# Tokens and first weights in quarters, column halves at the ends of stages, products of high parts at their beginnings, in a two-block fp32 model kernel

## The chip, the cores and the metric

One Trainium2 chip, of which the kernel uses one core. The metric is the device time of one execution in microseconds, median of a few runs. TensorE multiplies, VectorE and ScalarE work on elements, GpSimd does small odd jobs, SyncE issues most transfers. Each engine takes its instructions in order, and engines wait for each other on semaphores.

## What is computed

256 tokens of width 1024, all in float32, go through two models of two layers each. The first model: a convolution mixer, a gated linear recurrence, and after each a mixture of 16 experts of which a token takes 2. The second: forgetting attention (16 heads) and dilated attention (3 groups of 8 heads), and after each a feed-forward part with a width-3 convolution.

```python
for layer in (0, 1):                         # first model
    m = conv_mixer(x) if layer == 0 else rglru_mixer(x)
    x = layer_norm(4**0.25 * x + m)
    f = moe(x)        # softmax router, best group of 4, top 2; silu(x@w1) * (x@w3) @ w2
    x = layer_norm(4**0.25 * x + f)
h = rms_norm(x); x = x + forgetting_attention(h @ w_qkv, log_sigmoid(h @ w_f + b)) @ w_out
x = x + conv_ffn(rms_norm(x))                # second model
kv = rms_norm(x) @ w_kv; q = rms_norm(x) @ w_q
x = x + dilated_attention(q, kv) @ w_out
x = x + conv_ffn(rms_norm(x))
return rms_norm(x)
# conv_ffn: u = causal_conv3(h @ w_up) + b; a, g = split(u); (silu(g) * a) @ w_down
```

## The kernel before, in words

The work is a fixed sequence of stages: ew_in, ew_out (mixer of layer 0), moe0, ow_in, gates, ow_out (recurrence), moe1, aq/av, aw_out (attention), up0, down0, wk, bwq, wv, bw_out (dilated attention), up1, down1. All weights come from HBM once, in chunks of 1 MB (128 partitions x 2048 floats), 541 of them in the order of `STREAM` (L39). They go into a ring of 12 slots and 11 extra slots that other buffers leave free at times; `sync_load` (L303) has SyncE issue each load as soon as the slot's previous chunk is released (`released`, L283). For the experts the release is the last product with a chunk, for dense stages the split of its last quarter.

**Three products for one.** Dense stages keep float32 precision on a faster format: a weight piece of 512 columns (a quarter of a chunk) is rounded by ScalarE to a high part (`scalar_split`, L317, signal w_hi), and VectorE subtracts it to get the low part (`vector_split`, L325, w_lo). The activations are split likewise (x_hi, x_lo). `three` (L343) then multiplies low x high, high x low and high x high into one PSUM bank. Four pieces are held split; TensorE signals w_used for a piece, and only then the piece four further on may be split. `tensor_features` (L352) makes 256 output features of all tokens with a chunk: two halves j, each 8 x 3 = 24 products of 256 columns. `tensor_out` (L383) and, for its last part, `tensor_out_last` (L400) make an output projection with 512 columns a product: two token halves m, two column halves d. The last 24 products are the end of an output stage.

**Expert stages** multiply the float32 chunks directly (L1012), in the order in which they land.

**Between stages.** After ew_out and ow_out VectorE adds the residual by token half and column half (`vector_residual`, L611), gathers statistics and has GpSimd raise the variance to the power -0.5 (`pool_rstd`, L442); the halves are normalised (token half 0 on ScalarE, 1 on VectorE), turned by TensorE (`tensor_norm_features`, L495) and, ahead of od and fg, scaled and split in quarters q (`scalar_normed_split`, L553, and `vector_normed_split`, L568). Before the attention and feed-forward stages the factor of the rms norm goes onto a diagonal (`vector_rms`, L639, signal diag) and TensorE turns and scales at once (`tensor_to_features`, L508): token half 0, then half 1, into banks 4 to 7. The sum of squares comes from one ScalarE instruction over 1024 columns (`scalar_rms`, L629).

**The order around the change.** In the first stage SyncE loads x as two token halves (`sync_setup`, L676), then ten chunks; TensorE turns half 0, then half 1; ScalarE splits all four pieces of chunk 0 before it takes any high part of x, then VectorE the low parts; ScalarE also requests the constants `cols` (L670). At the beginning of any stage the first product waits for x_lo. In `forget_tensor` (L1767) the 24 products for the gate's logits come first and wait for all of x_lo. `vector_after_experts` (L1303) splits pieces 0 and 1, then does statistics and norm. In `tensor_out_last` the loop is m, then kk (the two contraction blocks), then d, so for each token half the first column half is done after 9 of 12 products. At the end `vector_finish` (L2478) applies factor and gain to a whole token half in one instruction, and `sync_store` stores it.

## Time and profile before

| | us |
|---|---|
| median of 3 runs (lowest, highest) | 1844.25 (1841.64, 1846.14) |
| the profiled execution's own time | 1845.43 |
| its span, first to last instruction | 1844.2 |
| TensorE busy in it | 1718.9 (93%) |
| VectorE busy | 797.8 (43%) |
| ScalarE busy | 614.8 (33%) |
| GpSimd busy | 119.8 (6%) |
| read from HBM | 542.19 MB, 295 GB/s over the span |

The busy share says how much of the span an engine had something in hand, not whether it set the pace: in the expert stages TensorE is busy nearly all the time and yet may run behind a stream of weights. For a question about one stage the stretch is to be read: who waits for whom there, the share of the DMA engines, and the clock that TensorE was granted (1.00 is 2.4 GHz, 0.50 is 1.2 GHz).

### The profile page before, as it was taken

To read this page: it belongs to the slowest core of one execution; us is meant where nothing else is said; L and a number is where in the kernel's file an instruction comes from. 1 tells how busy PE (TensorE), PEld (TensorE's weight loads), DVE (VectorE), ACT (ScalarE), POOL (GpSimd) and SP (SyncE) were. 2 spreads that over 40 slices of the span, in tenths; PEclk is the share of its full clock that TensorE was granted. 3 is DMA by queue.
4 is the path that set the end of the run, shared out by engine and by line. 5 is a ranking of instruction groups with operands and counts; after the bars stand their busy time and mean duration, and the time that the engine had idled before them with its cause. 6 is when DMAs were issued, how large, how long until landed. Compare 5 with 4: busy or idle time off the path is not lost.

```text
span 1844.2 us, 23747 instructions
## 1 busy us (share of the span) xinstructions
PE 1718.9 (93%) x9906; PEld 1115.7 (61%) x9906; DVE 797.8 (43%) x1534; ACT 614.8 (33%) x1157; POOL 119.8 (6%) x143
## 2 busy tenths in 40 slices
PE   8978999999997988999999988799999999999998
PEld 7954444333233974334432332777999889779986
DVE  5962111110003673111110001766788667758885
ACT  5531010000002551001000001456666554656664
POOL 0000000000000000000000000033111001501110
PEclk9989999999999988999999999999999999999999
DMA  9449999999999549999999999434455544335550
GB/s 398 186 189 377 423 422 422 424 423 420 420 419 419 225 168 383 424 422 424 421 422 423 420 420 420 187 123 144 147 184 182 193 159 163 125 125 184 183 183 24
DMA packets 75378, 544.88 MB, mean 295 GB/s; under 512 B 8448, under 2 KB 8448, under 8 KB 9472
## 3 DMA queue, kind: packets, MB, share of 16 engines
q1 hardware_dynamic: 74592, 541.10, 73.6%
q10 hardware_dynamic: 672, 2.18, 0.3%
q8 instruction: 82, 1.34, 0.3%
q14 instruction: 32, 0.26, 0.0%
HBM read 542.19 MB, written 1.05 MB: 295 GB/s over the span
## 4 chain that ended last, share of the span: by engine, by line
PE 68%; DMA 18%; DVE 8%; ACT 3%; issue 1%; POOL 1%; SPq 0%; ACTq 0%; DVEq 0%
PE PS L1012 24%; DMA ring<-in_w 12%; PE PS L346 12%; PE PS L348 11%; PE PS L347 11%; DMA F<-in_w 3%; PE PS L989 2%; PE PS L1024 2%; DVE wl L329 2%; DMA ring<-in_a_w_in 2%; DMA ring<-in_odd_w_in 1%; PE PS L737 1%; ACT wh L323 1%; DVE X L619 1%; PE PS L1038 0%
## 5 line engine op out<-in xcount | busy, mean ns | idle before, releaser
L1012 PE MATMUL PS<-ring,F 128*64 128x512 f32 x2112 | 477.7, 597 | 38.6 <-DMA ring<-in_w 33.8
L329 DVE TENSOR_TENSOR wl<-ring,wh 128x512 fp32r<-128x512 f32 x512 | 368.1, 739 | 189.5 <-ACT wh L323 186.8
L323 ACT ACTIVATE wh<-ring 128x512 fp32r<-128x512 f32 x512 | 319.8, 630 | 299.7 <-PE PS L348 292.0
L346 PE MATMUL PS<-xh,wl 128*128 128x256 f32 x1216 | 353.7, 291 | 10.7 <-DVE xl L834 3.8
L1012 PEld LDWEIGHTS PS<-ring,F 128*64 128x64 f32 x2112 | 143.6, 137 | 355.3 <-issue 258.9
L347 PE MATMUL PS<-xl,wh 128*128 128x256 f32 x1216 | 346.6, 285 | 0.0
L348 PE MATMUL PS<-xh,wh 128*128 128x256 f32 x1216 | 346.5, 285 | 0.0
L346 PEld LDWEIGHTS PS<-xh,wl 128*128 128x128 f32 x1216 | 235.5, 194 | 15.3 <-issue 5.7
L347 PEld LDWEIGHTS PS<-xl,wh 128*128 128x128 f32 x1216 | 235.7, 194 | 0.6
L348 PEld LDWEIGHTS PS<-xh,wh 128*128 128x128 f32 x1216 | 235.5, 194 | 0.0
L346 PE MATMUL PS<-wh,xl 128*128 128x512 f32 x360 | 148.1, 411 | 13.1 <-DVE xl L435 6.0
L348 PE MATMUL PS<-wh,xh 128*128 128x512 f32 x360 | 143.2, 398 | 0.0
L347 PE MATMUL PS<-wl,xh 128*128 128x512 f32 x360 | 143.1, 397 | 0.0
L1301 DVE COPY F<-PS 64x512 f32<-64x512 f32 x32 | 22.2, 695 | 270.7 <-PE PS L1012 270.7
L1280 DVE SCALAR_TENSOR_TENSOR F<-F,PS 128x512 f32<-128x512 f32 x32 | 22.0, 688 | 229.3 <-ACT F L1129 229.3
L1012 PE MATMUL PS<-F 128*64 128x512 f32 x480 | 109.3, 597 | 3.4 <-DMA F<-in_w 2.4
L1285 DVE SCALAR_TENSOR_TENSOR F<-F,PS 128x512 f32<-128x512 f32 x32 | 22.0, 688 | 205.3 <-PE PS L1012 205.3
L1147 ACT ACTIVATE F<-PS 64x512 f32<-64x512 f32 x32 | 18.9, 590 | 233.6 <-PE PS L1012 233.6
L1129 ACT ACTIVATE F<-PS 128x512 f32<-128x512 f32 x32 | 19.1, 597 | 231.6 <-PE PS L1012 231.6
L346 PEld LDWEIGHTS PS<-wh,xl 128*128 128x128 f32 x360 | 69.4, 193 | 32.3 <-DVE xl L435 11.8
L348 PEld LDWEIGHTS PS<-wh,xh 128*128 128x128 f32 x360 | 69.2, 192 | 15.2
L1141 ACT ACTIVATE F<-PS 128x512 f32<-128x512 f32 x32 | 19.0, 595 | 177.4 <-PE PS L1038 177.4
(353 smaller groups left out, 1760.6 us busy)
## 6 DMA issues: line engine op xcount, KB each, us to landing
ring<-in_w SPq DMA_DIRECT2D x264, 1024.0 KB, 26.4
F<-in_w SPq DMA_DIRECT2D x60, 1024.0 KB, 25.2
ring<-in_ffn_up SPq DMA_DIRECT2D x44, 1024.0 KB, 4.9
early<-in_w SPq DMA_DIRECT2D x40, 1024.0 KB, 25.8
ring<-in_ffn_down SPq DMA_DIRECT2D x22, 1024.0 KB, 4.8
ring<-in_even_w_in SPq DMA_DIRECT2D x10, 1024.0 KB, 17.0
Z<-in_w SPq DMA_DIRECT2D x10, 1024.0 KB, 23.4
XT<-in_w SPq DMA_DIRECT2D x10, 1024.0 KB, 24.1
```

The lines of the kernel that those rows point to most:

```text
L323: act.e.activation(self.wh[:, p % NPIECE, :], self.piece_source(p), ACT.Copy).then_inc(*self.up("w_hi", p))
L329: dve.e.tensor_tensor(self.wl[:, p % NPIECE, :], self.piece_source(p), f32(self.wh[:, p % NPIECE, :]), ALU.subtract).then_inc(*self.up("w_ ...
L346: e.matmul(out, left[1], right[0], start=first, stop=False)
L347: e.matmul(out, left[0], right[1], start=False, stop=False)
L348: return e.matmul(out, left[0], right[0], start=False, stop=last)
L989: t = pe.e.matmul(self.PS[:, 6 + half, k4 * 128:k4 * 128 + 128], self.X[:, h, k * 128:k * 128 + 128], v["S"][:, h, :], start=(h == 0), sto ...
L1012: t = pe.e.matmul(PS[64 * half:64 * half + 64, bank, :], lhs(k), weights[:, a:a + 512], start=(k == 0), stop=(k == 7))
L1024: t = pe.e.matmul(self.PS[:, b, :], v["Gt"][:, h, d, :], v["Y"][d], start=(q == 0), stop=(q == 7))
L1129: act.e.activation(v["hh"], PS[:, 4, :], ACT.Tanh, scale=0.5).then_inc(*up("tanh", layer, ex))
L1280: e.scalar_tensor_tensor(out=v["hh"], in0=v["hh"], scalar=1.0, in1=PS[:, 4, :], op0=ALU.add, op1=ALU.mult).then_inc(*up("silu", layer, ex))
L1285: e.scalar_tensor_tensor(out=v["hh"], in0=v["hh"], scalar=0.5, in1=PS[:, 5, :], op0=ALU.mult, op1=ALU.mult).then_inc(*up("hidden", layer, ex))
L1301: e.tensor_copy(v["Y"][1 - o][64:128, :], PS[64:128, 5, :]).then_inc(*up("y1", layer, ex))
```

## The change

Five edits.

1. **The start.** x comes as four column quarters of both token halves, chunk 0 as its four pieces, in the order tokens 0, piece 0, tokens 1 to 3, pieces 1 to 3, each on its own semaphore. TensorE turns quarter by quarter. ScalarE and VectorE split piece 0, take quarters 0 to 2 of x, piece 1, quarter 3, pieces 2 and 3. The constants are computed by VectorE after the split of piece 7 (in `constants`), not before that of piece 4. The first block of features goes to bank 6.
2. **First block of a stage.** With `first`, the 24 products of j = 0 run as 16 products with the high part of x (both weight parts), which wait for x_hi and w_lo, then 8 with its low part, which wait for x_lo. It is used at the beginnings of the first stage, od, fg, kv, up0 and up1; up0 and up1 use bank 0 for it. In fg the logits follow block 0.
3. **Splits ahead of od and fg.** ScalarE takes high part 1 before it normalises quarter 2. VectorE splits pieces 2 and 3 before and after the norm instead of between the low parts.
4. **Column halves.** `tensor_out_last` runs d outside kk, so a column half is done after 6 of 12 products. Squares are taken by column halves, and one VectorE instruction adds the two sums and epsilon. VectorE adds column half 0 of token half 1 before it waits for the factor of token half 0.
5. **The end.** VectorE multiplies by the gain before the factor is known; ScalarE applies the factor to columns 0 to 511, VectorE to the rest; four stores of 0.25 MB take the place of two of 0.5 MB.

```diff
-    def tensor_features(self, stage, p, bank):
+    def tensor_first_features(self, stage, p, out, xh, xl):
+        pe = self.pe
+        for k in range(8):
+            h, l = self.weight(p + k // 4)
+            a = slice(k % 4 * 128, k % 4 * 128 + 128)
+            pe.wait_ge(self.at("x_hi", stage, k // 2), self.at("w_lo", p + k // 4))
+            pe.e.matmul(out, l[:, a], xh[:, k, :], start=k == 0, stop=False)
+            pe.e.matmul(out, h[:, a], xh[:, k, :], start=False, stop=False)
+        for k in range(8):
+            h, l = self.weight(p + k // 4)
+            a = slice(k % 4 * 128, k % 4 * 128 + 128)
+            pe.wait_ge(self.at("x_lo", stage, k // 2))
+            t = pe.e.matmul(out, h[:, a], xl[:, k, :], start=False, stop=k == 7)
+            if k % 4 == 3:
+                t.then_inc(*self.up("w_used", p + k // 4))
+                yield p + k // 4
+    def tensor_features(self, stage, p, bank, first=False):
         pe, PS = self.pe, self.PS
         xh, xl = self.left.get(stage, (self.xh, self.xl))
         for j in range(2):
+            if first and j == 0:
+                yield from self.tensor_first_features(stage, p, PS[:, bank, 0:256], xh, xl)
+                continue
...
         for m in range(2):
             x = slice(m * 128, m * 128 + 128)
-            for kk in range(2):
-                k = nk - 2 + kk
-                for d in range(2):
+            for d in range(2):
+                for kk in range(2):
+                    k = nk - 2 + kk
...
         self.scalar_normed(stage, n, 0)
         high(0)
+        high(1)
         self.scalar_normed(stage, n, 2)
-        for q in (1, 2, 3):
-            high(q)
-    def vector_normed_split(self, stage, n, to, pieces):
+        high(2)
+        high(3)
+    def vector_normed_split(self, stage, n, to):
         dve = self.dve
         self.vector_normed(stage, n, 1)
         low(0)
         self.vector_normed(stage, n, 3)
-        low(1)
-        for p in pieces:
-            self.vector_split(p)
-        low(2)
-        low(3)
+        for q in (1, 2, 3):
+            low(q)
...
-        if src_stage:
-            act.wait_ge(self.at("resid", src_stage, h, 0), self.at("resid", src_stage, h, 1))
-        else:
-            act.wait_ge(self.at("x_final", h))
-        act.e.activation(self.Z[:, h, :], self.X[:, h, :], ACT.Square, scale=1.0 / 32,
-                         accum_out=self.sm[:, 430 + h:431 + h]).then_inc(*self.up("square", stage, h))
+        for d in range(2):
+            c = slice(d * 512, d * 512 + 512)
+            act.wait_ge(self.at("resid", src_stage, h, d) if src_stage else self.at("x_final", h))
+            act.e.activation(self.Z[:, h, c], self.X[:, h, c], ACT.Square, scale=1.0 / 32,
+                             accum_out=self.sm[:, 430 + 2 * h + d:431 + 2 * h + d]).then_inc(*self.up("square", stage, h, d))
+    def vector_rms_sum(self, stage, h):
+        self.dve.wait_ge(self.at("square", stage, h, 1))
+        self.dve.e.tensor_scalar(self.sm[:, 490 + h:491 + h], self.sm[:, 430 + 2 * h:431 + 2 * h],
+                                 self.sm[:, 431 + 2 * h:432 + 2 * h], RMS_EPS, ALU.add, ALU.add).then_inc(
+            *self.up("var_eps", (stage, h)))
     def vector_rms(self, stage, h):
         dve = self.dve
-        dve.wait_ge(self.at("square", stage, h))
-        self.vector_rstd(self.sm[:, 430 + h:431 + h], RMS_EPS, h, (stage, h))
         dve.wait_ge(self.at("rstd", (stage, h)))
         dve.e.tensor_scalar(self.Z[:, h, 0:128], self.ident[:, :], self.sm[:, 500 + h:501 + h], None,
                             ALU.mult).then_inc(*self.up("diag", stage, h))
+    def vector_out_rms(self, stage, p, nk):
+        self.vector_residual(stage, p, nk, 0, 1.0, self.X)
+        self.vector_rms_sum(stage, 0)
+        self.vector_residual(stage, p, nk, 1, 1.0, self.X, halves=(0,))
+        self.vector_rms(stage, 0)
+        self.vector_residual(stage, p, nk, 1, 1.0, self.X, halves=(1,))
+        self.vector_rms_sum(stage, 1)
+        self.vector_rms(stage, 1)
...
     def sync_setup(self):
-        for h in range(2):
-            self.sp.e.dma_start(self.X[:, h, :], self.A["x"][h * 128:h * 128 + 128, :]).then_inc(self.x_in[h][0], 16)
+        x, w = self.A["x"].rearrange("(h p) d -> p h d", h=2), self.source(0)
+        def tokens(q):
+            s = slice(256 * q, 256 * q + 256)
+            self.sp.e.dma_start(self.X[:, :, s], x[:, :, s]).then_inc(self.x_in[q][0], 16)
+        def piece(j):
+            s = slice(PIECE * j, PIECE * j + PIECE)
+            self.sp.e.dma_start(self.chunk(0)[:, s], w[:, s]).then_inc(self.first_in[j][0], 16)
+        tokens(0)
+        piece(0)
+        for q in (1, 2, 3):
+            tokens(q)
+        for j in (1, 2, 3):
+            piece(j)
...
+        pe.wait_ge(at("consts", "ident"))
+        for q in range(4):
+            pe.wait_ge(self.x_in[q])
+            for h in range(2):
+                for j in range(2):
+                    k = 2 * q + j
+                    t = pe.e.transpose(PS[:, q, j * 256 + h * 128:j * 256 + h * 128 + 128],
+                                       self.X[:, h, k * 128:k * 128 + 128], self.ident[:, :])
+            t.then_inc(*up("turned", "ev", q))
         p, conv = PIECES["ew_in"], 0
         for c in range(10):
             if c < 4:
-                pe.wait_ge(at("x_lo", "ev", c))
+                pe.wait_ge(at("x_hi" if c == 0 else "x_lo", "ev", c))
             elif c >= 6:
                 pe.wait_ge(self.even_bank_read((0, 1, 4, 5)[c - 6]))
-            for _ in self.tensor_features("ev", p + 4 * c, (0, 1, 2, 3, 4, 5, 0, 1, 4, 5)[c]):
+            for _ in self.tensor_features("ev", p + 4 * c, (6, 1, 2, 3, 4, 5, 0, 1, 4, 5)[c], c == 0):
...
     def even_scalar(self):
         act, at, up, v = self.act, self.at, self.up, self.even_views()
-        for n in range(NPIECE):
+        for q in range(4):
+            if q in (0, 3):
+                self.scalar_split(q // 3)
+            act.wait_ge(at("turned", "ev", q))
+            act.e.activation(self.xh[:, 2 * q:2 * q + 2, :], self.bank2(q), ACT.Copy).then_inc(*up("x_hi", "ev", q))
+        for n in (2, 3):
             self.scalar_split(n)
         self.scalar_setup()
-        for q in range(4):
-            act.wait_ge(at("turned", "ev", q))
-            act.e.activation(self.xh[:, 2 * q:2 * q + 2, :], self.bank2(q), ACT.Copy).then_inc(*up("x_hi", "ev", q))
...
-        for n in range(NPIECE):
-            self.vector_split(n)
         for q in range(4):
+            if q in (0, 3):
+                self.vector_split(q // 3)
             dve.wait_ge(at("x_hi", "ev", q))
             dve.e.tensor_tensor(self.xl[:, 2 * q:2 * q + 2, :], self.bank2(q), f32(self.xh[:, 2 * q:2 * q + 2, :]),
                                 ALU.subtract).then_inc(*up("x_lo", "ev", q))
-        dve.wait_ge(self.cols_in)
-        dve.wait_ge(at("ev_pad"), at("ev_consts", "bh"))
+        for n in (2, 3):
+            self.vector_split(n)
+        def constants():
...
+                if (c, j) == (0, 3):
+                    constants()
...
             self.vector_moments(stage, h)
+        self.vector_split(p + 2)
         self.vector_norm(stage)
+        self.vector_split(p + 3)
...
-        pe.wait_ge(at("wf_lo"))
-        for k in range(8):
-            pe.wait_ge(at("x_lo", "fg", k // 2), at("x_lo", "fg", 3))
-            a = slice(k * 48, k * 48 + 48)
-            t = self.three(PS[0:48, 7, 0:256], (self.wfh[:, a], self.wfl[:, a]), (self.xh[:, k, :], self.xl[:, k, :]),
-                           k == 0, k == 7)
-        t.then_inc(*up("fg_logits"))
         p0 = self.forget_slots()
         for c in range(2):
-            for p in self.tensor_features("fg", p0 - 8 + 4 * c, c):
+            for p in self.tensor_features("fg", p0 - 8 + 4 * c, c, c == 0):
                 self.forget_tensor_slot(p - p0)
+            if c == 0:
+                self.forget_logits()
...
+        if stage != "down1":
+            for h in range(2):
+                self.scalar_rms(stage, stage, h)
+            return
+        self.scalar_rms(stage, stage, 0)
+        self.scalar_finish(0)
+        self.scalar_rms(stage, stage, 1)
+        self.scalar_finish(1)
...
+    def ffn_bank(self, n):
+        return 4 + n % 4 if n else 0
...
+            pe.wait_ge(at("taps", layer, n - 4) if n >= 4 else at("x_lo" if n else "x_hi", stage, n))
+            for _ in self.tensor_features(stage, p + 4 * n, self.ffn_bank(n), n == 0):
...
-    def vector_finish(self, h):
+    def vector_finish(self, p, nk):
         dve, at, up = self.dve, self.at, self.up
-        dve.wait_ge(at("square", "down1", h))
-        self.vector_rstd(self.sm[:, 430 + h:431 + h], RMS_EPS, h, ("down1", h))
-        dve.wait_ge(at("rstd", ("down1", h)), (self.s_row, 48))
-        dve.e.scalar_tensor_tensor(out=self.Z[:, h, :], in0=self.X[:, h, :], scalar=self.sm[:, 500 + h:501 + h],
-                                   in1=self.F[:, 12288:13312], op0=ALU.mult, op1=ALU.mult).then_inc(*up("y_ready", h))
+        G = self.F[:, 12288:13312]
+        def gain(h, d):
+            c = slice(d * 512, d * 512 + 512)
+            dve.wait_ge((self.s_row, 48), at("resid", "down1", h, d), at("square", "down1", h, d))
+            dve.e.tensor_tensor(self.Z[:, h, c], self.X[:, h, c], G[:, c], ALU.mult).then_inc(*up("y_gain", h, d))
+        def scale(h):
+            dve.wait_ge(at("rstd", ("down1", h)), at("y_gain", h, 1))
+            dve.e.tensor_scalar(self.Z[:, h, 512:1024], self.Z[:, h, 512:1024], self.sm[:, 500 + h:501 + h], None,
+                                ALU.mult).then_inc(*up("y_ready1", h))
+        self.vector_residual("down1", p, nk, 0, 1.0, self.X)
+        self.vector_rms_sum("down1", 0)
+        gain(0, 0)
+        gain(0, 1)
+        self.vector_residual("down1", p, nk, 1, 1.0, self.X, halves=(0,))
+        scale(0)
+        self.vector_residual("down1", p, nk, 1, 1.0, self.X, halves=(1,))
+        gain(1, 0)
+        self.vector_rms_sum("down1", 1)
+        gain(1, 1)
+        scale(1)
...
+    def scalar_finish(self, h):
+        act, at, up = self.act, self.at, self.up
+        act.wait_ge(at("rstd", ("down1", h)), at("y_gain", h, 0))
+        act.e.activation(self.Z[:, h, 0:512], self.Z[:, h, 0:512], ACT.Copy,
+                         scale=self.sm[:, 500 + h:501 + h]).then_inc(*up("y_ready0", h))
     def sync_store(self):
         for h in range(2):
-            self.sp.wait_ge(self.at("y_ready", h))
-            self.sp.e.dma_start(self.out[h * 128:h * 128 + 128, :], self.Z[:, h, :]).then_inc(self.s_out, 16)
-        self.sp.e.wait_ge(self.s_out, 32)
+            for d in range(2):
+                c = slice(d * 512, d * 512 + 512)
+                self.sp.wait_ge(self.at(f"y_ready{d}", h))
+                self.sp.e.dma_start(self.out[h * 128:h * 128 + 128, c], self.Z[:, h, c]).then_inc(self.s_out, 16)
+        self.sp.e.wait_ge(self.s_out, 64)
...
```

## Rows read from the trace of the kernel before

**Rows 1.** Page, part 4: the chain that ended last, by engine
```profile
PE 68%; DMA 18%; DVE 8%; ACT 3%; issue 1%; POOL 1%; SPq 0%; ACTq 0%; DVEq 0%
```

**Rows 2.** Stretches: busy by engine (count); last three: TensorE's clock, DMA share, GB/s
```profile
60.00:116.00 56.00, 50.03 (x306) 44.99 (x305) 45.05 (x96) 27.44 (x52) 0.72 (x1) 0.93 0.22 76
150.00:152.00 2.00, 2.00 (x12) 0.72 (x10) 0.00 (x0) 0.00 (x0) 0.00 (x0) 1.00 0.09 37
158.00:580.00 422.00, 402.21 (x1896) 150.57 (x1892) 48.44 (x109) 39.22 (x68) 0.00 (x0) 1.00 1.01 421
...
718.00:720.00 2.00, 2.00 (x11) 0.62 (x8) 0.00 (x0) 0.00 (x0) 0.00 (x0) 1.00 0.56 90
722.00:1151.00 429.00, 405.32 (x1904) 151.25 (x1904) 50.03 (x113) 37.04 (x65) 0.42 (x1) 1.00 1.01 419
...
600.00:610.00 10.00, 10.00 (x85) 10.00 (x85) 6.68 (x13) 6.16 (x11) 0.00 (x0) 1.00 0.99 411
```

**Rows 3.** Timeline, first 20 us: start, us, engine, line, operation, count [idle <- releaser]
```profile
4.63 3.64 PE L524 MATMUL PS<-ident,X 128*128 128x128 f32 x16 [4.63 <-DMA X<-in_x]
8.26 0.63 ACT L323 ACTIVATE wh<-ring 128x512 fp32r<-128x512 f32 x1 [6.17 <-DMA ring<-in_even_w_in]
12.07 0.58 PE L346 MATMUL PS<-xh,wl 128*128 128x256 f32 x1 [3.80 <-DVE xl L834]
16.55 0.17 DVE L837 TENSOR_SCALAR sm<-cols 128x4 f32<-128x4 f32 x1 [2.74 <-DMA cols<-in_cols]
```

**Rows 4.** Stretches as in rows 2, around beginnings of stages, for the clock
```profile
12.07:16.10 4.03, 4.03 (x19) 4.03 (x20) 1.74 (x3) 0.95 (x2) 0.00 (x0) 1.00 1.01 422
593.10:599.95 6.85, 6.55 (x29) 6.29 (x30) 3.79 (x6) 1.49 (x3) 0.00 (x0) 0.50 1.02 420
1163.40:1169.90 6.50, 4.72 (x23) 4.41 (x24) 3.99 (x5) 0.00 (x0) 0.00 (x0) 0.50 0.57 205
1487.20:1494.00 6.80, 4.22 (x33) 3.75 (x33) 4.14 (x10) 4.08 (x10) 0.76 (x2) 1.00 0.03 13
```

**Rows 5.** Timeline of VectorE, end of ew_out
```profile
123.87 0.69 DVE L621 SCALAR_TENSOR_TENSOR Z<-X,PS 128x512 f32<-128x512 f32 x1 [0.78 <-PE PS L348]
```

**Rows 6.** Timeline, beginning of od
```profile
587.37 1.53 DVE L474 TENSOR_SCALAR Z<-PS,sm 128x512 f32<-128x512 f32 x2 [0.68 <-POOL sm L444]
593.01 1.29 DVE L329 TENSOR_TENSOR wl<-ring,wh 128x512 fp32r<-128x512 f32 x2
591.67 1.66 ACT L560 ACTIVATE xh<-XT 128x512 fp32r<-128x512 f32 x3
587.84 1.97 PE L503 MATMUL PS<-ident,Z 128*128 128x128 f32 x16 [2.48 <-ACT Z L492]
597.54 0.41 PE L348 MATMUL PS<-xh,wh 128*128 128x256 f32 x1
```

**Rows 7.** Timeline of TensorE, beginning of fg
```profile
1165.18 0.42 PE L346 MATMUL PS<-xh,wfl 128*48 128x256 f32 x1 [5.91 <-DVE xl L575]
```

**Rows 8.** Timeline, end of down0: first and last of its last 24 products, then the tail
```profile
1481.74 0.39 PE L346 MATMUL PS<-wh,xl 128*128 128x512 f32 x1
1486.95 0.39 PE L348 MATMUL PS<-wh,xh 128*128 128x512 f32 x1
1489.07 2.02 PE L522 MATMUL PS<-Z,X 128*128 128x128 f32 x16 [1.73 <-DVE X L619]
1491.36 2.05 PE L522 MATMUL PS<-Z,X 128*128 128x128 f32 x16 [0.27 <-DVE Z L644]
1483.98 1.37 DVE L619 TENSOR_TENSOR X<-X,PS 128x512 f32<-128x512 f32 x2 [0.68 <-PE PS L348]
1491.02 0.29 DVE L644 TENSOR_SCALAR Z<-ident,sm 128x128 f32<-128x128 f32 x1 [0.67 <-POOL sm L444]
```

**Rows 9.** Timeline, the last instruction of VectorE; and the store's time to landing
```profile
1840.21 1.28 DVE L2483 SCALAR_TENSOR_TENSOR Z<-X,sm,F 128x1024 f32<-128x1024 f32 x1 [0.67 <-POOL sm L444]
DMA to landing us min/median/max: 2.6/2.6/2.6
```

70 lines of the change are left out of this document (35 added, 35 removed).

## The prediction

> **What bounds the kernel now.** I began with the chain that ended last: 68% of the span is TensorE and 18% DMA [rows 1]. The reader should then ask, stretch by stretch, which of the two sets the pace. In the stretches of the experts the DMA share is full for 422 and 429 us at 421 and 419 GB/s [rows 2]: whatever TensorE gains inside them is worth nothing, and they move only if the stream of weights begins earlier. Between them and after them the stream is nearly idle or has room (0.22 of it is used at 60 to 116 us [rows 2]), and TensorE and the small chains between two stages set the time. The change touches only those: the first 20 us, the ends of stages, and their beginnings.
>
> Does a gain ahead of an expert stretch reach the end? The stream stalls just before each saturated stretch, because every slot is full until the first expert frees one: 0.91 of 150 to 152 us is idle (1.8 us), and 0.44 of 718 to 720 us (0.9 us) [rows 2]. All its later loads are released by TensorE's progress. So what the even and the odd stage gain moves the whole stream, and what only the tail between the last fill and the first expert gains (0.68 us, below) fits into those idle times. I count both in full.
>
> **The first stage.** Now: the first half of the tokens (0.5 MB) lands at 4.6 us, the first weight chunk (2 MB in all by then) at 8.2 us, TensorE turns tokens for 3.64 us and then idles 3.80 us until the first low part of x exists, at 12.07 [rows 3]. With eight transfers of 0.25 MB in the order of the diff, and the same rate (1.5 MB in 3.6 us, so 0.6 us for a quarter), tokens land at 4.0, 5.2, 5.8, 6.4 and the pieces at 4.6, 7.0, 7.6, 8.2 us. Sixteen transposes at 3.64/16 = 0.23 us, four for a quarter, end at 8.0 us (TensorE is the late one, not the DMA). The high parts and piece 0's split hide under them: ScalarE and VectorE have nothing else there. Products then start at about 8.1 instead of 12.07: 4.0 us. Further, the clock. The rows print a granted clock of 1.00 from the start, but 19 products took 4.03 us at 12.07 (0.212 each) [rows 4], where transposes of later stages go at 1.97/16 = 0.12 [rows 6]: the first is the pace of 1.2 GHz, the second that of 2.4. The pace rose after 4.03 us of unbroken work. In the new order TensorE is busy without a break from 5.2 us (second quarter), so I let it rise at 9.3 us: 6 slow products instead of 19, 13 x 0.09 = 1.2 us. Sum 5.2 us. Bounds: 2 us, if the smaller transfers are a good deal slower, and 6 us.
>
> The Trainium skill speaks to this: "TensorE: Matmul & The Clock Gate", section "Part 1: The HAM clock gate", says that the warm-up is an amount of time with activity and not a number of matmuls. By that rule it is right that the transposes count; if only the products counted, the 1.2 us would go.
>
> What it adds: the request for the constants (cols) now stands behind the fourth split in ScalarE's queue, which waits for piece 3 (8.2 us, where it now waits for the chunk, 8.2 us as well), so it goes out when it did and lands near 16.5 us as before [rows 3]. VectorE meets that wait after the split of piece 7 instead of before that of piece 4. Behind it stands piece 8, due when TensorE ends the second block of columns at about 20 us; cover 2.5 us. Pieces 0 and 1 are given back at products 20 and 24 instead of 12 and 24; their successors are needed at product 48, 28 x 0.12 = 3.4 us later, and a release costs two splits, some 2 us. Both at nothing; gone, each would cost about 1 us per us late.
>
> **The ends of ew_out and ow_out (column halves one by one).** VectorE is the late one: from 123.87 us, when the first half is done [rows 5], it has sums and statistics without a gap (as the timeline goes on) up to the factor of the norm. In the last 24 products the first half is done after 6 instead of 9. At (1486.95 - 1481.74)/23 = 0.2265 us for a product [rows 8] the whole VectorE chain starts 0.68 us earlier; its second half is due after 12 products as before, which then just meets it. Twice 0.68 = 1.4 us. The piece with number 2 is now wanted after 3 products instead of 6; it was split two pieces' time before, and I find some room. Cost 0, at worst 0.3 each (half a split).
>
> **The beginnings of od and fg.** In od transposes end at 589.81 (587.84 + 1.97); ScalarE ends the last high parts at 593.3, the 24th product starts at 597.54 [rows 6]. The two weight splits that stood between the low parts go elsewhere: one into the 0.68 us in which VectorE waits for GpSimd ahead of the norm [rows 6] (the pair in the way took 1.29, so one fits: free), one into the wait for the transposes. ScalarE's sum is unchanged, so the last high part comes at 593.4, 12 products are left then, and VectorE's low parts, with no splits between, follow the high parts by one operation of some 0.7 and are ready at 594.3, before they are due. At 0.12 us the 24 are done at 594.9, 2.9 us earlier than 597.75, and 10 products that ran slow before 599.95 run fast: 3.7 us. But the granted clock was 0.50 in 593.10 to 599.95 [rows 4], after a thin stretch from 589.81. If it falls again, the 24 are done at 593.4 + 12 x 0.212 = 595.95: 8.5 products ahead, 1.0 us if it rises when it did, 2.3 if sooner; I take 1.5.
>
> In fg TensorE idles 5.91 us until 1165.18, as the logits of the forget gate want all low parts, and then runs 23 products in 6.5 us at a clock of 0.50 [rows 4, 7]. Now block 0 comes first, on high parts, and the logits second, so 24 products are done by 1159.27 + 3.6 (as in od) + 12 x 0.12 = 1164.3, where the 24th used to end near 1170: 5.5 us. If the clock falls: 1165.4, and at 1169.9 about 23 products ahead, x 0.12 = 2.8; I take 3.0. Nothing of block 1 is late by it: behind the low parts VectorE multiplies in the gains as before, now some 5 us earlier.
>
> Does the clock fall? Before, the thin stretch was 3.3 us empty but for 6 products, then two more waits (od), and 5.9 us empty (fg). Now it is 3.5 us with 12 to 16 products in it in each. That is about as thin as what held the clock elsewhere (the rms tails, idle for 1.73 us [rows 8], kept 1.00 [rows 4]). I take it that it falls in one of the two: 3.7 + 3.0 or 1.5 + 5.5, so 6.9 us.
>
> **The three rms tails (aw_out, down0, bw_out) and the beginnings behind them.** Now VectorE adds token half 0 at 1483.98 (0.43 after the start of the 9th product), waits for its square and factor, and only then adds half 1, so TensorE starts turning at 1489.07 though the last product started at 1486.95 [rows 8]. New: half 1's last column half is added at 1486.95 + 0.43, 0.69 long (half of 1.37): 1488.07; TensorE starts 0.15 later, 1488.22, and is through half 0 after 2.02 us at 1490.24. The factor of half 1 took 2.1 us from the sum to its diagonal (1489.07 - 0.15 to 1491.02 [rows 8]); squaring halves as they come shortens that, so it is there by 1490.1. TensorE itself is then the late one: 1491.36 becomes 1490.24, 1.12 us. Behind it the first block starts on high parts, but VectorE's splits of pieces 2 and 3 still follow the low parts, as in the code of before, and are due at the end of the 24: 0.2 us. Three times 1.32 = 4.0 us.
>
> **The end (down1).** Now the last factor is applied in 1.28 us from 1840.21 and the store takes 2.6 us from issue to landing [rows 9]. New: the last sum ends about 0.6 us earlier (VectorE has gains to multiply in between), the factor is applied by two engines to half a row each (0.6 instead of 1.28, gain 0.7), and the last store is half as large (0.6 us less to move) but is the second of two issued together (0.35 later). Sum 0.6 + 0.7 + 0.3 = 1.6 us; bounds 0.5 and 2.5. The skill's "DMA: Bandwidth & Descriptors", section "Anatomy of one DMA", fits 2.0 us plus the bytes at 436 GB/s to a transfer; an estimate by that page puts the half store 0.6 us below the whole, as I do.
>
> **Sum.** 5.2 + 1.4 + 6.9 + 4.0 + 1.6 = 19.1 us. The profiled execution took 1845.4 (span 1844.2 and 1.2 around it), 1.2 over the median of the three; it would come to 1826.3, the median to 1844.25 - 19.1 = 1825.
>
> **Rivals.** (a) The clock holds in od and fg: 3.7 + 5.5, so 21.4 and 1823. (b) It falls in both: 4.5, so 16.7 and 1827.5. (c) Small transfers are slower, 1.0 us a quarter: the start gives 3, 1827. (d) They don't overlap at all. Each of the eight takes the 2.6 us that a store shows [rows 9]; the last piece lands at 22 us, block 0 ends at 25 instead of 19.6, and the start loses 5.4: 1835.7. For it: nothing in the trace; against it: 2 MB by 8.2 us [rows 3] is full overlap. It is what the rule to batch transfers to 1 MiB or more in the skill's "DMA: Bandwidth & Descriptors", section "Measured (HBM→SBUF, 128 partitions, SWDGE, issued from GpSimd)", would make of it at its worst. (e) The heads bring nothing, since low parts or splits are as late as before (the diff doesn't do what it says): minus 7.5, 1832.6. Against it: the splits between the low parts are gone. (f) The expert stream doesn't move: all gains ahead of it are lost (5.2 + 1.4 + 2.6): 1834.3. Against it: its idle times in [rows 2]. (g) Slower: the stream, always full, settles at a lower rate, because the loads meet TensorE's releases in another rhythm. It covers 851 us; it eats the 19.1 and 5.5 more from 851/(851 + 24.6) x 420 = 408 GB/s on. Ten microseconds in a later full part show 411 [rows 2], so such a rate exists; none lasts.
>
> **How the numbers follow.** A measurement of this kernel tells some 0.3% (5.5 us) from no change. Chances: forecast 0.38, (a) 0.24, (b) 0.18, (c) 0.06, (d) 0.02, (e) 0.05, (f) 0.05, (g) 0.02. All but (g) lie under 1838.7, so faster 0.96, same 0.02, slower 0.02. Range: from 1821 (a, with 2 us for the spread of runs and the upper bounds) to 1832 (b and c with the lower bounds of start and end, and half of e): 0.86 or so.
>
> **What would show it.** The first product at about 8 us and block 1 at 14.4 instead of 19.6; the first expert product some 6 us earlier; the same DMA share in the expert stretches; 24 products done 3.6 + 1.4 us after the transposes in od and fg, with the granted clock beside it; transposes of the rms tails 0.85 us nearer to the last product, and no wait between their halves. It would be wrong if VectorE's wait for the constants reached past 19 us, if a low part turned up as releaser of more than 0.3 us in a beginning, or if the rate of the stream changed.

## The result and the profile after

| | kernel before | kernel after |
|---|---|---|
| median of the runs | 1845.2 us (4 runs, 1841.6 to 1847.3) | 1829.3 us (4 runs, 1826.4 to 1830.8) |
| profiled execution | 1845.4 us (span 1844.2) | 1828.6 us (span 1827.3) |
| mean granted clock in it | 0.985 | 0.987 |

The ratio is 0.9917 (0.9898 to 0.9935): 16 us faster, under 1%, but clear of the spread of the runs. Over all later comparisons, before has a median of 1843.6 us in 35 runs, so 14 to 16 us is the better statement. The forecast was 19.1 us less and a median of 1825, in a range of 1821 to 1832.

Where the two profiled executions reach the same instruction of TensorE (us; lead is how much earlier after is there, new is what it gained since the row above):

| what starts | before | after | lead | new |
|---|---|---|---|---|
| first convolution | 32.75 | 29.55 | 3.2 | 3.2 |
| routing of layer 0 | 133.03 | 127.75 | 5.3 | 2.1 |
| second gather, behind 16 expert products | 153.24 | 149.74 | 3.5 | -1.8 |
| last combination of layer 0 | 581.68 | 578.63 | 3.05 | -0.45 |
| od's first recurrence product | 630.40 | 624.23 | 6.2 | 3.1 |
| routing of layer 1 | 699.59 | 691.25 | 8.3 | 2.2 |
| second gather, layer 1 | 719.81 | 713.23 | 6.6 | -1.8 |
| last combination of layer 1 | 1151.26 | 1144.75 | 6.5 | -0.1 |
| fg, first turning of attention weights | 1205.65 | 1194.37 | 11.3 | 4.8 |
| turning behind down0 | 1489.07 | 1475.58 | 13.5 | 2.2 |
| end of the span | 1844.2 | 1827.3 | 16.9 | 3.4 |

Every change shows where it was made, and in two places time is given back: at the first expert of each layer. TensorE's timeline in the trace of after, at the start of the kernel, where it answers [rows 3], and from the routing of layer 0 to the first expert (start, us, engine, line, operation, count, [idle <- releaser]):

```profile
3.71 1.09 PE L782 MATMUL PS<-ident,X 128*128 128x128 f32 x4 [3.71 <-DMA X<-in_x]
7.34 2.82 PE L782 MATMUL PS<-ident,X 128*128 128x128 f32 x12 [2.54 <-DMA X<-in_x]
9.81 0.56 PE L361 MATMUL PS<-xh,wl 128*128 128x256 f32 x1
13.71 0.28 PE L348 MATMUL PS<-xh,wl 128*128 128x256 f32 x1
...
137.69 0.40 PE L1132 MATMUL PS<-sm,upper 128*128 128x16 f32 x2 [3.57 <-DVE sm L1273]
139.44 3.78 PE L1056 MATMUL PS<-F,X 128*128 128x128 f32 x16
143.91 5.89 PE L1079 MATMUL PS<-F 128*64 128x512 f32 x16 [0.69 <-ACT F L1182]
```

The same place in before:

```profile
142.98 0.61 PE L1065 MATMUL PS<-sm,upper 128*128 128x16 f32 x2 [3.58 <-DVE sm L1206]
149.66 3.65 PE L1012 MATMUL PS<-F 128*64 128x512 f32 x16 [0.69 <-ACT F L1115]
```

The second quarter of the tokens was there only at 7.3 us, where I had 5.2. And the 16 first expert products took 5.89 us instead of 3.65: TensorE idles for 3.6 us in the routing in both kernels, and the granted clock is 0.50 behind it; in before it was back at 1.00 as the expert began, in after it was not. TensorE busy, granted clock, DMA share and GB/s by two microseconds, before and then after:

```profile
148.00:150.00 2.00, 1.31 (x7) 0.65 0.96 406
150.00:152.00 2.00, 2.00 (x12) 1.00 0.09 37
```

```profile
142.00:144.00 2.00, 1.31 (x8) 0.50 1.04 438
144.00:146.00 2.00, 2.00 (x6) 0.50 0.61 258
146.00:148.00 2.00, 2.00 (x6) 0.50 0.02 8
148.00:150.00 2.00, 2.00 (x10) 0.88 0.62 152
```

### The profile page after: what moved, and what is told of

Same layout as the page of the kernel before. It is cut to its first block, busy times and chain, and to the rows that moved or that the text cites. A ratio compares the mean times of both kernels' runs of the same rounds, so it can differ in the third digit from the quotient of the medians.

```text
span 1827.3 us, 23779 instructions
## 1 busy us (share of the span) xinstructions
PE 1717.2 (94%) x9906; PEld 1111.1 (61%) x9906; DVE 799.2 (44%) x1538; ACT 619.0 (34%) x1179; POOL 121.2 (7%) x143
## 3 DMA queue, kind: packets, MB, share of 16 engines
q8 instruction: 82, 1.34, 0.3%
## 4 chain that ended last, share of the span: by engine, by line
PE 70%; DMA 18%; DVE 6%; ACT 3%; issue 1%; POOL 1%; SPq 1%; DVEq 0%; ACTq 0%
PE PS L1079 24%; DMA ring<-in_w 12%; PE PS L348 12%; PE PS L350 11%; PE PS L349 11%; DMA F<-in_w 3%; PE PS L1056 2%; PE PS L1091 2%; DMA ring<-in_a_w_in 2%; DMA ring<-in_odd_w_in 1%; DVE wl L331 1%; PE PS L795 1%; ACT wh L325 1%; PE PS L545 1%; SPq L313 1%
## 5 line engine op out<-in xcount | busy, mean ns | idle before, releaser
L348 PE MATMUL PS<-xh,wl 128*128 128x256 f32 x1168 | 336.4, 288 | 2.7 <-ACT F L1645 1.4
L349 PE MATMUL PS<-xl,wh 128*128 128x256 f32 x1168 | 330.4, 283 | 0.0
L350 PE MATMUL PS<-xh,wh 128*128 128x256 f32 x1168 | 330.3, 283 | 0.0
L348 PEld LDWEIGHTS PS<-xh,wl 128*128 128x128 f32 x1168 | 223.8, 192 | 5.9 <-issue 2.3
L349 PEld LDWEIGHTS PS<-xl,wh 128*128 128x128 f32 x1168 | 223.9, 192 | 0.6
L350 PEld LDWEIGHTS PS<-xh,wh 128*128 128x128 f32 x1168 | 223.9, 192 | 0.0
L1196 ACT ACTIVATE F<-PS 128x512 f32<-128x512 f32 x32 | 19.1, 597 | 236.3 <-PE PS L1079 236.3
L348 PEld LDWEIGHTS PS<-wh,xl 128*128 128x128 f32 x360 | 69.0, 192 | 32.3 <-DVE xl L458 11.9
L350 PEld LDWEIGHTS PS<-wh,xh 128*128 128x128 f32 x360 | 68.9, 191 | 15.1
```

Of the source, the lines that this page charges most:

```text
L348: e.matmul(out, left[1], right[0], start=first, stop=False)
L349: e.matmul(out, left[0], right[1], start=False, stop=False)
L350: return e.matmul(out, left[0], right[0], start=False, stop=last)
L1196: act.e.activation(v["hh"], PS[:, 4, :], ACT.Tanh, scale=0.5).then_inc(*up("tanh", layer, ex))
```

## The experiments

Times within a kernel are read from its one profiled execution; medians are of 4 to 10 runs, beside runs of before on the same chip.

**The start alone.** Before, with the start of after.

> The kernel before with the new start alone (tokens and first weights by quarters, block 0 on high parts first). Theory (the start is worth 3.2 us, and what it gains travels on, less what a clock that is still low takes back): the first convolution product 3.2 us earlier than before (29.7 instead of 32.9), the first expert product 3 to 5 us earlier than 149.66, and the end 1 to 4.8 us earlier, by whether the 16 first expert products take 3.65 us (granted clock back at 1.00) or up to 5.9 (still 0.50). Rival (the stream of expert weights does not move): the end 0 us earlier, with the first expert waiting for a transfer. Rival (it loses in the hand-over to the next stages): the lead at 104 us is under 3.2.

1840.2 us against 1842.5 (ratio 0.9986, 0.9973 to 1.0): by the medians alone the start is worth 0 to 5 us. Within the profiled execution it is plainer. First convolution at 29.52, as in after. First expert at 143.63, six us early, since the clock also kept its 1.00 ahead of the middle of the stage; 16 products in 3.65 us; last combination of layer 0 at 576.28: 5.4 us early. The lead passes through the stream of expert weights. That holds in every kernel tried: from the second gather to the last combination it took 428.2 to 429.6 us in layer 0, for second gathers between 145.3 and 153.2 us.

**Why the start gives 3.2.** Three other ways to load the first 2 MB:

```diff
 e_tok2k:  tokens(0), tokens(1), piece(0), tokens(2), tokens(3), piece(1..3)
+    h, s = q % 2, slice(q // 2 * 512, q // 2 * 512 + 512)   # 2 KB rows
+    dma_start(self.X[:, h, s], x[:, h, s])
 e_tok4k:  tokens by half (4 KB rows) x2, then piece(0..3)   # 2 KB rows
 e_rows4k: tokens by half (4 KB rows) x2, then two pieces at a time (4 KB rows) x2
```

> The kernel after with the tokens still in four transfers of 0.25 MB, but each a token half by a column half (2 KB rows) instead of both token halves by 256 columns (1 KB rows), in the order two, piece 0, two, pieces 1 to 3. Theory (short rows slow the queue down to 100 to 130 GB/s between 3.3 and 5 us): the second pair lands by 5.8 instead of 7.3, the first product starts at about 8.6 instead of 9.8, and the first convolution 1 us earlier than 29.7. Rival (small transfers start slowly whatever their rows, or several share the engines): first product at 9.6 to 10, convolution within 0.3 us of 29.7.

> The kernel after with the tokens in two transfers of 0.5 MB again (one for each token half, 4 KB rows), both ahead of the first weights, which stay in four pieces; the rest as after. Runs so far: 1 KB rows moved at 100 to 130 GB/s from 3.3 to 5 us, 2 KB rows at 170 to 250, and the 4 KB rows of before at 430. Theory (a row costs its engine about the same time whatever its length, so short rows are what took 2 us from the start): the rate is at 400 or more from 3.3 us on, all tokens are there by 6.5 us, TensorE turns them without a gap to 8.4 us, the first product starts near 8.4 and the first convolution near 28.3 instead of 29.55: 1 to 1.3 us gained. Rival (the first weights are then too late): piece 0 lands after 8 us and the first product starts at 9.5 or later, nothing gained.

> The kernel after with rows of 4 KB for all that is loaded first: tokens in two transfers (one for each token half), then the first chunk in two (two pieces each), nothing under 0.5 MB. Runs so far: the rate of the queue fell to 80 to 180 GB/s whenever transfers with rows of 1 or 2 KB began, and was 420 while the 4 KB rows of the tokens moved. Theory (row length): no such dip, 400 GB/s or more from 3.5 us on; tokens there by 6, pieces 0 and 1 by 7.2, 2 and 3 by 8.3 us; first product by 8.6 and no wait for a split behind it; first convolution at 28.3 to 28.9 instead of 29.0 to 29.75. Rival (the dip belongs to the first weights, whatever their rows): it comes again at 5 us, first product at 9.2, a wait behind it, convolution near 32.

The rate of the queues in the first 12 us, 40 slices of 0.3 us, GB/s; before, after, e_tok4k, e_rows4k:

```profile
GB/s 0 0 0 0 0 0 246 55 109 218 355 437 437 437 396 423 382 464 437 410 437 437 382 437 437 437 437 437 437 437 437 437 410 410 437 437 437 410 437 379
```

```profile
GB/s 0 0 0 0 0 0 34 188 362 382 290 130 82 133 116 102 123 219 266 304 335 352 324 294 328 283 236 300 355 396 423 464 457 505 437 437 437 437 410 437
```

```profile
GB/s 0 0 0 0 0 0 27 109 191 314 423 423 410 423 396 423 369 225 253 157 116 164 123 191 225 300 348 362 376 444 437 464 444 437 410 437 437 410 437 410
```

```profile
GB/s 0 0 0 0 0 0 109 177 164 137 341 437 410 423 423 423 437 382 396 341 232 218 341 382 382 423 478 464 451 437 437 410 437 437 437 437 437 437 437 437
```

The dip stands where the first weights begin, not where the short rows of the tokens are. In after the first tokens, in 1 KB rows, moved at 362 to 382 GB/s up to 3.0 us. In the dip (114 GB/s from 3.3 to 5.1 us) most of the bytes are those of piece 0, in 2 KB rows, and from 5.1 to 7.2 us the 1 KB rows of the other tokens moved at 299 GB/s. In e_tok4k the dip comes with the weights' 2 KB rows (176 GB/s from 5.1 to 7.2 us), in e_rows4k with their 4 KB rows (225 from 6.0 to 6.6), and in before, with 8 KB rows, not at all. So the theory that I took into these runs, that the tokens' 1 KB rows are the slow ones, falls. Its rival in the last of them, that the dip belongs to the first weights, holds, with the addition that it is the weaker the longer their rows are. What makes it is open. Outside the dip the length of a row has a small price: a packet of 1, 2, 4 and 8 KB took its engine 46, 84, 159 and 309 ns, which is 356, 390, 412 and 424 GB/s for 16 engines.

The time did not follow the rate. The first product came earlier than the 9.81 us of after, at 9.58 (2 KB tokens), 9.19 and 9.14 us, but the first convolution at 29.75, 32.12 and 30.23 us, where the kernels with the start of after have 28.98 to 29.55; the medians are 1830.1, 1829.4 and 1829.9. In the last two the first piece lands behind all tokens (ScalarE's split at 7.70 and 7.64 instead of 5.79), its low part is what TensorE waits for (1.24 and 0.93 us), and so is that of piece 1 (1.21 and 0.35), which stands in VectorE's queue behind three low parts of x. The clock did more. TensorE's timeline in e_tok4k; then its busy time, granted clock, DMA share and GB/s by four microseconds there, and last the same in after:

```profile
9.19 0.36 PE L361 MATMUL PS<-xh,wl 128*128 128x256 f32 x1 [1.24 <-DVE wl L331]
11.59 0.56 PE L361 MATMUL PS<-xh,wl 128*128 128x256 f32 x1 [1.21 <-DVE wl L331]
```

```profile
8.00:12.00 4.00, 1.60 (x10) 0.86 1.03 421
12.00:16.00 4.00, 4.00 (x21) 0.50 1.02 426
16.00:20.00 4.00, 4.00 (x29) 0.78 1.01 416
```

```profile
12.00:16.00 4.00, 4.00 (x36) 1.00 0.99 416
```

In after the pace was low from the first product, 9.81, to 11.9 us, and then high. In e_tok4k it was high at the first product, fell to 0.50 at 10.9 and came back at 17.7 us. That is 6.1 us of work at half the pace (from 11.59 on) against 2.1, so 2.0 us lost; with the wait of 1.2 and less the start that came 0.6 earlier it makes the 2.6 by which the convolution is late. In e_rows4k, where the pace rose at 13.5 us, the same sum is 0.9 + 0.35 - 0.7, for the 0.7 measured. What the order of after gives is that TensorE works without an idle time from 7.34 us on; that the waits of 1.2 us are what made the clock fall is argued from their place ahead of it.

**Undoing the beginnings, and undoing the ends.** e_heads_old is after with `first` false everywhere but in the first stage, the forget gate's logits ahead of block 0, and splits of pieces 2 and 3 between the low parts; e_tails_old is after with whole-row squares, `for kk ... for d` in the last products of ew_out and ow_out, and the old last scaling and stores.

> The kernel after with the old beginnings of od, fg, the first up products and kv (block 0 waits for low parts, two weight splits between the low parts, the forget gate's logits first); everything else as after. Theory (they are worth 3.1 in od, 4.8 in fg and 0.2 in each of the other three): the run loses 8.5 us, 1838. Of the 1.35 to 1.43 us per rms tail and head, 0.1 to 0.3 is lost. Rival (the beginnings matter little, the gain at od and fg is the clock that fell elsewhere): it loses under 4 us, with the same 24 products in the same time.

> The kernel after with the old ends: squares of whole rows, the factor of half 0 ahead of half 1's sums, the old order in the last products of ew_out and ow_out, the old last scaling and the two whole stores. Theory (0.68 at each of ew_out and ow_out, 1.1 to 1.2 at each of three rms tails, 1.4 at the end): 6.3 us lost, 1835.5. Rival (the tails are worth less, since low parts are what is waited for behind them either way): the 24 products of the next stage start later but end within 0.5 us, and 3 us are lost. Rival (the clock of 0.50 at the first expert products hides what ew_out and ow_out gained): 1.4 of it shows up as nothing, 5 us lost.

Medians 1834.8 us (1833.7 to 1837.0) and 1833.4 us (1830.3 to 1841.2): 5.4 and 4.1 lost, where 8.5 and 6.3 were expected. Runs with this spread can't tell the 6.3 of the ends from their rivals' 5 and 3, so the places decide: fg, from its first transpose to its first decay product, takes 32.3 to 32.5 us in the three kernels with the old beginning and 27.2 to 27.8 in eight of ten with the new one (the others, with fillers, took 28.9 and 30.3, the latter with a stand-still as below): 4.8 us, as expected. od, from its transposes to its first recurrence product, takes 40.8, 42.6 and 43.8 us old, and 38.9 to 41.5 new in all but one run with a stand-still: 2.5 between the means, with the clock fallen in both kinds. In the one pair that differs in the beginnings alone, e_heads_old and after, od differs by 1.3 only (40.8 and 39.5), and with fg's 4.8 and the heads below that makes up the 5.9 us between their profiled executions. So fg's part is sure, and od's lies between 1.3 and the 3.1 of the table. From the turning behind aw_out to that behind down0, one tail and one head, 195.60 us in before, 194.20 in after, 195.43 with the old tails, 194.29 with the old heads: the tail is worth 1.2 to 1.3, the head 0.1 to 0.2. The tail in after, and with the old ends:

```profile
1474.38 0.29 DVE L669 TENSOR_SCALAR Z<-ident,sm 128x128 f32<-128x128 f32 x1
1475.58 3.92 PE L545 MATMUL PS<-Z,X 128*128 128x128 f32 x32 [0.87 <-DVE X L640]
1477.10 0.29 DVE L669 TENSOR_SCALAR Z<-ident,sm 128x128 f32<-128x128 f32 x1 [0.67 <-POOL sm L467]
```

```profile
1485.12 2.02 PE L545 MATMUL PS<-Z,X 128*128 128x128 f32 x16 [1.72 <-DVE X L640]
1487.41 2.05 PE L545 MATMUL PS<-Z,X 128*128 128x128 f32 x16 [0.27 <-DVE Z L665]
```

0.85 us less ahead of the 32 transposes and 0.27 less between them, the 1.12 of the working. The two ends of ew_out and ow_out gave their 0.68 us each: the idle time ahead of the norm's transposes is 1.34 in after and 2.02 in e_start_only and in e_tails_old.

**Holding the clock.** TensorE turns the identity (or multiplies it by ones) into bank 7, which nobody reads, instead of idling.

```diff
+    def tensor_fill(self, n):            # e_fill, e_fill_start, e_route_fill
+        for _ in range(n):
+            self.pe.e.transpose(self.PS[:, 7, 0:128], self.ident[:, :], self.ident[:, :])
+    def tensor_fill(self):               # e_route_long, e_both
+        for _ in range(7):
+            self.pe.e.matmul(self.PS[:, 7, 0:256], self.ident[:, :], self.ones[:, :], ...)
 moe_tensor_route, ahead of the wait for "chosen":
+        self.tensor_fill(27)             # 30 in e_route_fill
 tensor_norm_features("ln1"), ("ln3"):
+        self.tensor_fill(18)             # e_fill and e_fill_start only
```

> The kernel after with TensorE turning the identity into a bank that nobody reads while it would wait: 27 such transposes in each routing (behind the tokens' transposes), 18 ahead of the norm's transposes for od and for fg. Theory (the time given back at the first experts, and the slow beginnings of od and fg, are the clock that fell in those waits): the granted clock stays at 1.00 there; the gather takes 2.0 instead of 3.8 us, the first 16 expert products 3.65 instead of 5.89 and 5.61, the norm's transposes 1.97 instead of 3.14 and 2.83, and fg's 24 first products 2.2 us less. Up to 4.7 us in each routing, 1 in od, 3 in fg: 13 us below the kernel after, some 1816. Rival 1 (transposes of one small operand do not hold the clock): same time as after, 1829, clock still 0.50. Rival 2 (the clock holds, but the stream of expert weights is then what is late): expert products wait for transfers, and only od's and fg's 4 us are left, 1825.

> As the run before, and TensorE also turns the identity 8 times before the first tokens land and 9 times before the second quarter. Theory (the pace of 1.2 GHz up to 11.9 us is a clock that had not risen yet, since TensorE idled 2.5 us between the quarters): the 12 transposes of the last three quarters take 1.5 instead of 2.8 us, the first product comes at about 8.6 instead of 9.8, the 24 are done at 11.5 instead of 13.7; 2 us below the run before. Rival (the clock rises at a fixed time after the start, whatever TensorE does): nothing gained, 0 us. Rival (the filler delays the tokens' transposes): 0.3 to 0.5 us slower at the first product.

> The kernel after with 30 transposes of the identity in each routing alone (none ahead of od and fg, where the two runs with fillers stood still for 2.4 to 3.7 us with nothing to wait for but the next instructions). Theory (fillers hold the clock, what took the gain back was that stand-still): granted clock 1.00 from 133 to 160 and from 696 to 720, first expert products over 4 us earlier than after in layer 0 (by 145.4 instead of 149.8), 3 to 4 more in layer 1, no idle time put down to issue at 580 and 1150; 1829.3 less 6 to 8, some 1822. Rival (the stream of expert weights takes it back): leads over after at 578 and 1145 us under 1 us, 1828 or more. Rival (the stand-still moves elsewhere): a wait for issue of over 1 us in some other stage.

> The kernel after with seven long products (identity by ones, 256 columns of four-byte numbers, 0.45 us each) in each routing in place of the 30 short transposes: the same 3.2 us of work for TensorE in a quarter of the instructions. In the run with 30 short ones TensorE stood still for 4.5 us in the middle of the transposes for od, behind the branch that skips the overflow path, with all it waited for done. Theory (it was the next block of instructions that came late: the added instructions moved its edge from where TensorE waits anyway into work): with few instructions no wait for issue over 1 us, clock 1.00 at the first experts, 1829.3 less 4 to 7: 1822 to 1825, and the fastest executions near 1819. Rival (the stand-still comes from the higher activity of TensorE, not from the count of instructions): a wait for issue of over 2 us near 580 or 1150 again, 1827 to 1829. Rival (seven long products are no activity that holds the clock): 0.50 at the first experts, 1829.

> The two runs before in one kernel: rows of 4 KB first, and seven long products in each routing. Theory (the one gains 0.5 to 1 us at the start, the other 4 to 7, and both reach the end, since the stream of expert weights took 428.2 to 429.6 us from the first expert's second gather on, at leads from 0 to 8 us): 1821 to 1824. Rival (the stream's time grows by what comes ahead of it): within 1 us of the kernel after, 1829.

Medians in this order: 1830.5, 1828.9, 1827.5 (1819.8 to 1831.2), **1822.9** (1821.1 to 1823.9) and 1825.9 us. Against the expectations: e_fill missed its 1816 by 14.5 us, e_fill_start gained 1.6 over it where 2 were expected, e_route_fill's third rival came (the stand-still moves elsewhere), e_route_long's theory came in full, and e_both lies between its theory and its rival. The clock was held as expected behind the filler in the routing of layer 0: in e_fill the first expert's gather took 2.05 us and its 16 products 3.65, a gain of 4.4 over after by 145.31. But the gain was gone by 590 us. TensorE's timeline of e_fill, e_route_fill and e_route_long behind the last combination of layer 0:

```profile
580.61 2.06 PE L520 MATMUL PS<-ident 128*128 128x128 f32 x12 [2.72 <-issue]
586.40 1.54 PE L520 MATMUL PS<-ident 128*128 128x128 f32 x6 [3.73 <-issue]
```

```profile
580.96 1.36 PE L530 MATMUL PS<-ident,Z 128*128 128x128 f32 x9 [2.38 <-ACT Z L515]
586.80 1.75 PE L530 MATMUL PS<-ident,Z 128*128 128x128 f32 x7 [4.47 <-issue]
```

```profile
581.94 2.27 PE L530 MATMUL PS<-ident,Z 128*128 128x128 f32 x16 [2.34 <-ACT Z L515]
585.05 0.39 PE L361 MATMUL PS<-xh,wl 128*128 128x256 f32 x1 [0.84 <-ACT xh L587]
```

Here the program has a branch that skips the overflow path, and the stream fills the queues. Fillers that wait for nothing start 2.4 to 2.7 us late, and then TensorE stands still for 3.7 and 4.5 us in the middle of ready work (2.5 us at 1152 us in e_fill_start). "Runtime: NRT & Kernel Launch", section "Instruction fetch mechanics", of the Trainium skill says that instructions come in blocks through a queue of their own, and that a taken branch to a block not at hand has to fetch it first. The traces agree in that idle times over 1 us named "issue" occur behind this branch only, in either layer; that it is a block's edge, moved by the 60 instructions (30 transposes with their weight loads) of a routing, is argued from e_route_long, where nearly the same busy time (3.2 us instead of 3.4) in seven products, which the trace lists as 14, had none. It is not shown more directly.

In e_both the start is 1.6 us later (first convolution 30.90 instead of 29.31, with the clock at 0.50 from 11.7 to 15.1 us, much as in e_tok4k); its stream took 429.2 us from the second gather, as the others did. The rest of its 3 us over e_route_long goes with a lower mean clock (0.989 against 0.991).

**What the clock does to one kernel.** Executions of the same kernel differ by up to 11 us, and their mean granted clock with them. Over all 95 executions of 13 kernels, within a kernel, 0.001 more of clock is 1.31 us less (standard error 0.09, correlation -0.85). By that slope, at a clock of 0.987: before 1841.6, the start alone 1838.3, beginnings undone 1833.4, ends undone 1833.3, after 1828.6, e_route_long 1828.3. So the parts are worth 3.3, 4.8 and 4.6 (each good to about 1 us), together 12.7 of the 13.0 between the kernels, and e_route_long gains by the clock alone (0.991 against 0.987). The kernels with short fillers come to 1836.6 (e_fill), 1835.2 (e_fill_start) and 1830.7 (e_route_fill): what they gained in clock they paid in stand-stills. That the clock is itself a result of idle time makes this a way of taking luck out, not a second measurement.

## Why the prediction was right, and where not

The median lies 4.3 us above the forecast and inside the range. By its steps (the profiled executions differ by 3.2 + 1.4 + 2.9 of clock ahead of the two routings + 7.9 in od and fg - 3.6 - 0.5 + 4.2 + 1.4 = 16.9):

- **The start: 5.2 forecast, 3.2 measured.** The mechanism was right, the transfer time was mis-sized: I gave eight transfers of 0.25 MB the rate of those of 0.5 and 1 MB. They moved at 82 to 133 GB/s for 1.8 us as the first weights began. That is rival (c), and its price was exact (the start gives 3). The first product came at 9.81 instead of 8.1, 1.7 of the missing 2.0; the pace rose some 2 us behind it instead of 1.2, and the 24 were done at 13.7. TensorE had worked since 7.34 us when the pace rose at 11.9, so the transposes counted, as I had taken it. Filling TensorE's waits there (e_fill_start) made the pace rise before the first product and end the 24 at 12.9, but at the first convolution it was 0.4 us ahead of after, and kernels with one and the same start differ by 0.6 there. Rival (d), no overlap, did not come. The wait for the constants held VectorE to 19.1 us, just past the 19 that I had named as a sign of being wrong, but TensorE waited for nothing behind it.
- **The ends of ew_out and ow_out: 1.4 forecast, 2 x 0.68 measured** in the idle time. The rest of the 2.1 and 2.2 in the table is clock: ahead of the two routings it was at 0.50 for 10.2 and 13.7 us in before, for 6.8 and 6.8 in after.
- **od and fg: 6.9 forecast, 7.9 between the profiled executions (3.1 + 4.8), of which od's share may be as low as 1.3.** The number came near by luck. I had the clock fall in one of the two; it fell in both, in after: the norm's transposes took 3.14 and 2.83 instead of 1.97 us, and in fg it stayed at 0.50 to 1158.8. Rival (b) priced fg at 3.0 for that case, which was too low: the low stretch began ahead of the first products and was over by 1159, so that it slowed fewer of them; in od it was over at 588.8, 0.4 us behind the first product. The 24 were done 4.6 us after the transposes' end in od (587.9 to 592.55; I had 5.0) and 5.7 in fg. And the split that I called free, in VectorE's wait for GpSimd, was not: beside it GpSimd's power took 0.94 instead of 0.56 us in od and 0.93 in fg (0.56 again in e_heads_old, which has no split there), and VectorE's norm began 0.38 us later behind the addition of epsilon. Whether that reached TensorE the traces don't separate. Before, then after:

```profile
586.77 0.56 POOL L444 TENSOR_TENSOR sm<-sm,mhalf 128x1 f32<-128x1 f32 x1 [0.51 <-DVE sm L440]
```

```profile
583.54 0.68 DVE L331 TENSOR_TENSOR wl<-ring,wh 128x512 fp32r<-128x512 f32 x1
583.71 0.94 POOL L467 TENSOR_TENSOR sm<-sm,mhalf 128x1 f32<-128x1 f32 x1 [0.51 <-DVE sm L463]
```

- **Tails and heads: 3 x 1.32 forecast, 1.35, 1.40 and 1.43 measured**, and e_heads_old and e_tails_old divide them as the working did.
- **The end: 1.6 forecast, 1.4 measured.** GpSimd's power took 0.93 us instead of 0.55 (below), more than the missing 0.2. The stores took 2.1 us to landing instead of 2.6, so 0.5 of the 0.6 said.
- **The stream: passed on, as said.** Rivals (f) and (g) fall: 420 and 419 GB/s in the two stretches, 421 and 419 before.
- **What no step had: the first experts, -3.6 us.** I treated TensorE's clock at the beginnings that I moved, and read none at those that I did not. The profiled execution of before had 1.00 at the first expert products of both layers, as e_start_only had; in the twelve such places of the six kernels built from after without filler, the 16 products took 3.65 us in four and 5.4 to 6.1 in eight. What decides it stands in the 16 routings without filler: where the clock fell 0.3 to 0.7 us ahead of the end of the idle time, it was back 6.2 to 6.5 us behind that end, in time for the expert products; where it fell between 0.1 us ahead of the end and 0.9 behind, it was back only after 10 to 11 us; in two, where it fell 0.9 and 1.5 us behind, it was back after 4.4 and 4.9. A shift of half a microsecond makes the difference, and this speaks for chance; whether the new order favours the late fall is open. The Trainium skill ("TensorE: Matmul & The Clock Gate", "Part 1: The HAM clock gate") says that the window in which activity is looked at runs free, so that the same kernel has a different number of slow products from run to run; the spread above agrees. It shows in the middle of the first stage: the same idle time of 2.15 us is followed by 0.50 in before and e_fill_start and left 1.00 in after.

## What to carry to other kernels

Sum a chain of small edits from the rows of each place and check each place afterwards: here the ends of stages came out within 0.2 us of their terms. The start missed by 2.0, where a transfer's rate was carried over to smaller transfers, and od and fg came near by two errors that offset each other. A TensorE kernel with idle times of 1 to 4 us has a clock term of several us that no single profile fixes, so compare mean clocks along with times, and look at what follows each idle time, also where nothing was changed. Filling the longest such wait with a few long products was worth another 6.5 us (1829.3 to 1822.9), while the same filler in many short instructions gave most of it back (1827.5).

## What the runs showed of the hardware

- The granted clock falls in every routing (3.6 us idle) without filler, and comes back 4 to 11 us after work resumes; with filler it stayed at 1.00 in layer 0 in all five kernels, and in layer 1 in four.
- Behind a branch, while weights stream, TensorE starts ready work 2.4 to 2.7 us late, and with 27 or 30 transposes added to the routing ahead it stood still for another 2.5 to 4.5 us in the middle, in three of six places (idle time named "issue").
- A packet of 1, 2, 4 and 8 KB from HBM took its engine 46, 84, 159 and 309 ns. The rate dips as the first small transfers of weights begin: 114 GB/s for 1.8 us with 2 KB rows in after, 225 for 0.6 us with 4 KB rows in e_rows4k.
- GpSimd's power on 128 numbers: 0.54 to 0.57 us alone and beside VectorE's statistics or additions out of PSUM, 0.92 to 0.94 us beside a multiplication or a split of 128x512 on VectorE, wherever one stands in the 13 traces. The last of after:

```profile
1822.81 0.68 DVE L2564 TENSOR_TENSOR Z<-X,F 128x512 f32<-128x512 f32 x1
1822.97 0.93 POOL L467 TENSOR_TENSOR sm<-sm,mhalf 128x1 f32<-128x1 f32 x1 [2.87 <-DVE sm L661]
1823.93 0.72 ACT L2586 ACTIVATE Z<-Z,sm 128x512 f32<-128x512 f32 x1 [1.29 <-POOL sm L467]
1823.94 0.49 DVE L2568 TENSOR_SCALAR Z<-Z,sm 128x512 f32<-128x512 f32 x1 [0.45 <-POOL sm L467]
```
